# Chunks of the split inputs begin 1088 bytes apart instead of 1024

## The reference, cut to what matters

```python
proj = h @ w_in[l]                                    # and so for each projection
a = jnp.einsum('cd,ced->ce', hc, u[ic])               # PEER, first half
return jnp.einsum('ce,ced->cd', a, v[ic])             # PEER, second half
u, gate_in = jnp.split(hn @ w_in, 2, axis=-1)         # feed-forward
return (jax.nn.gelu(c, approximate=False) * u) @ w_out
```

## Time and profile before

| | |
|---|---|
| runs | 2029.96, 2028.71, 2020.91 us; median 2028.71 |
| span of the profiled execution | 2021.6 us (its time outside the span isn't given; the median is 7.1 us above the span) |
| PE, PEld | busy 1877.1 us (93%), 1800.7 us (89%), 16,518 instructions each |
| DVE, ACT | busy 1456.5 us (72%), 1242.6 us (61%) |
| DMA | 296 MB, mean 146 GB/s |
| mean granted TensorE clock | 0.975 of full speed |

### The profile page before, as it was taken

One profiled execution on the slowest core, in us unless ns is written; L12 is line 12 of the kernel. 1 busy time (PEld: TensorE's weight loads), 2 busy tenths in 40 slices (PEclk: granted clock), 3 DMA queues, 4 the chain that ended last, 5 costly groups with the idle time before them and its releaser, 6 DMA issues. The chain is left out here.

```text
span 2021.6 us, 45016 instructions
## 1 busy us (share of the span) xinstructions
PE 1877.1 (93%) x16518; PEld 1800.7 (89%) x16518; DVE 1456.5 (72%) x3046; ACT 1242.6 (61%) x2420; POOL 0.2 (0%) x4
## 2 busy tenths in 40 slices
PE   8998988999999999999999989687999977999997
PEld 8887888999999976899999989587999976899996
DVE  7667667688985479766666667776888678578857
ACT  5454655777776789655555556733665555666555
POOL 0000000000000000000000000000000000000000
PEclk9999999999999999999999999798999989999998
DMA  6533344466655620266666646101665644166562
GB/s 208 158 97 105 118 143 136 132 194 193 179 186 175 186 84 0 84 194 190 196 191 193 193 139 199 52 3 56 184 196 173 192 126 136 34 190 189 176 198 76
DMA packets 102084, 296.06 MB, mean 146 GB/s; under 512 B 9539, under 2 KB 32454, under 8 KB 101830
## 3 DMA queue, kind: packets, MB, share of 16 engines
q1 hardware_dynamic: 101958, 294.35, 47.0%
HBM read 293.26 MB, written 1.05 MB: 146 GB/s over the span
## 5 line engine op out<-in xcount | busy, mean ns | idle before, releaser
L459 DVE TENSOR_TENSOR w_low<-ring,w_high 128x512 fp32r<-128x512 f32 x1102 | 743.2, 685 | 357.1 <-ACT w_high L453 349.2
L503 PE MATMUL bank<-a_high,w_high 128*128 128x256 f32 x3228 | 921.2, 285 | 74.3 <-DVE w_low L459 39.1
L504 PE MATMUL bank<-a_low,w_high 128*128 128x256 f32 x3228 | 907.5, 281 | 0.0
L505 PE MATMUL bank<-a_high,w_low 128*128 128x256 f32 x3228 | 907.4, 281 | 0.0
L453 ACT ACTIVATE w_high<-ring 128x512 fp32r<-128x512 f32 x1102 | 671.4, 624 | 375.3 <-PE bank L505 372.8
L503 PEld LDWEIGHTS bank<-a_high,w_high 128*128 128x128 f32 x3228 | 620.0, 192 | 90.0 <-DVE w_low L459 39.7
L504 PEld LDWEIGHTS bank<-a_low,w_high 128*128 128x128 f32 x3228 | 616.3, 191 | 0.4
L505 PEld LDWEIGHTS bank<-a_high,w_low 128*128 128x128 f32 x3228 | 616.7, 191 | 0.0
L503 PE MATMUL bank<-s_high,w_high 128*128 128x256 f32 x1024 | 283.5, 277 | 2.0 <-DVE s_low L2446 2.0
L504 PE MATMUL bank<-s_low,w_high 128*128 128x256 f32 x1024 | 283.3, 277 | 0.0
L505 PE MATMUL bank<-s_high,w_low 128*128 128x256 f32 x1024 | 283.3, 277 | 0.0
(11 more groups left out here) (368 smaller groups left out, 1867.8 us busy)
## 6 DMA issues: line engine op xcount, KB each, us to landing
ring<-in_stream SPq DMA_DIRECT2D x273, 512.0 KB, 3.7
ring<-in_peer_u SPq DMA_DIRECT2D x128, 512.0 KB, 3.6
ring<-in_peer_v SPq DMA_DIRECT2D x128, 512.0 KB, 3.5
ring<-in_stream SPq DMA_DIRECT2D x32, 256.0 KB, 3.3
ring<-in_stream SPq DMA_DIRECT2D x12, 192.0 KB, 2.7
x<-in_x SPq DMA_DIRECT2D x4, 256.0 KB, 6.3
arena<-in_mem SPq DMA_DIRECT2D x1, 1024.0 KB, 11.0
out<-x SPq DMA_DIRECT2D x4, 256.0 KB, 2.6
```

Of the source, the lines that this page charges most:

```text
L459: self.nc.vector.tensor_tensor(self.cut(h, self.w_low), self.raw(h), self.cut(h, self.w_high.bitcast(F32)), ALU.subtract)\
L503: self.nc.tensor.matmul(to, lh, rh, start=start, stop=False, **more)
L504: self.nc.tensor.matmul(to, lh, rl, start=False, stop=False, **more)
L505: return self.nc.tensor.matmul(to, ll, rh, start=False, stop=stop, **more)
```

## The change

The row of the tensors for split inputs gets 16 more floats, so that a chunk begins 1088 bytes behind the one before; the views that the kernel uses keep the shape of 256 tokens. 1088 is 2 times 512 and 64 more, so chunks 0 to 7 begin at eight different places modulo 512, 64 bytes apart. The weights' slots are as before. To make place for the longer rows (22 rows of 64 bytes), the arena of the hybrid room gets 256 floats fewer; its scratch moves down by these 1024 bytes.

```diff
+STRIDE = T + 16
-HYBRID_ROOM = 31488
+HYBRID_ROOM = 31232
@@ def pairs(self, chunks):
-        shape = [P, chunks, T]
-        with self.nc.sbuf_tensor(f"a_high{self.rooms}", shape, F32R) as self.a_high, \
-                self.nc.sbuf_tensor(f"a_low{self.rooms}", shape, F32R) as self.a_low:
+        shape = [P, chunks, STRIDE]
+        with self.nc.sbuf_tensor(f"a_high{self.rooms}", shape, F32R) as high, \
+                self.nc.sbuf_tensor(f"a_low{self.rooms}", shape, F32R) as low:
+            self.a_high, self.a_low = high[:, :, 0:T], low[:, :, 0:T]
             yield
@@ def peer(self):
-            with self.nc.sbuf_tensor("s_high", [P, SIDES, T], F32R) as s_high, \
-                    self.nc.sbuf_tensor("s_low", [P, SIDES, T], F32R) as s_low:
-                self.expert_sum(s_high, s_low)
+            with self.nc.sbuf_tensor("s_high", [P, SIDES, STRIDE], F32R) as s_high, \
+                    self.nc.sbuf_tensor("s_low", [P, SIDES, STRIDE], F32R) as s_low:
+                self.expert_sum(s_high[:, :, 0:T], s_low[:, :, 0:T])
```

## The result

| | before | after |
|---|---|---|
| median of four runs | 2028.82 us (2020.91 to 2029.96) | 2065.01 us (2064.09 to 2065.93) |
| ratio | | 1.0173, 95% interval 1.0136 to 1.021 |
| span of the profiled execution | 2021.6 us | 2062.3 us |
| mean granted clock | 0.975 | 0.975 |

A forecast was written before the change was run, and what follows sets the result against it. PE's own pace in the long products was taken to bound the kernel. Instructions, the ACT and DVE writers and PE's streams each counted 0 us, so the time stayed where the runs are: 2027 us, range 2006 to 2056.

The forecast's parts named there:

- the two gears: Lasting paces of PE's matmuls in the long products: fast at 113.3 ns, slow at 117.8 ns, changing where PE has stopped.
- two of its signs: Trace signs named beforehand: PEER's second half slower than 113.3 ns without a stall; a pace going with the chunk's number.
- The second rival: Long fast stretches on PE lose the 113.3 ns pace; whole 30 to 40 us more, 2059 to 2069 us; chance 0.22.
- the choice between the ends: For PE's streams, 0 us was taken between 16.8 us less and at most 40 us more.
- the term of the streams on PE: Effect of the new chunk starts on matmuls streaming while the next weights load; taken as 0 us.
- the last quarter of the loss: Top part of the at most 40 us loss on PE, left out of the range, which stopped at 2056 us.
- The first rival: Slow stretches on PE run at 113.3 ns because shifting relations end a lasting collision; 17 us less, 2012 us; chance 0.26.
- If no stretch at 117.8 is left: Sign in PE's stretches that was to show the slow gear going, 17 us less, as right.
- The second rival's mechanism: On PE, a constant relation keeps streams collision-free; seven of eight new relations put their meeting mid-stream; 30 to 40 us.
- The third rival: Spread starts on PE bring paces below the fast gear, by another 4.45 ns; 74 us less, 1955 us; chance 0.04.
- a draw of gears: A new allocation may bring other gears at some 110 restarts of PE's stream, scattering the time by 6 to 8 us.

The follow-up runs named there:

- low_128: Against the kernel before: a_high and s_high stay at relation -64, a_low and s_low start 128 bytes later, at +64; 2054.26 us, ratio 1.0129.

## Why the prediction was wrong

**Right:** what bounds the kernel, the two gears of the kernel before and their distance of 4.45 ns, that no operation of ACT, DVE or a queue changes, and that a change of pace in the long products would reach the path whole. The sums and the rows hold, and so do two of its signs: PEER's second half left 113.3 ns without a stall, and a pace went with the number of the chunk. The second rival, "the fast gear goes", is what happened, with 2059 to 2069 us for 2065.01 measured. That its 40 us meet the 40.7 of the spans so closely is partly luck: it took 4.45 ns where 5.0 came, gave nothing to the slow stretches, which lost 2.4 us, and counted matmuls outside the long stretches that are fast in no row.

**The step that failed** is the choice between the ends, by which the term of the streams on PE was put at 0: "Whatever tells the gears apart is therefore something in the timing of the start, and the one thing that the change alters is the same in both." The rows were read right: one set of addresses shows both gears. What followed from it was less than I took. It shows that the address does not choose between the two gears; it says nothing on which gears an address allows. The runs showed the term at 35 us in the long stretches alone, of 40.7 us of span: 32.6 us in the fast ones, 5.0 ns for each of some 6,610 matmuls, and 2.4 us in the slow ones. The relation of the kernel before is the only one of the six multiples of 32 tried, modulo 256, where 113.3 is common; of the four that the change visits the other three hardly allow it, and where a place of `s` comes back to the good one for 24 matmuls, the stream stays at 117.8. The prediction even said it: "No row shows another relation under this load". Where no row shows the new state, a forecast of 0 between a bound of -17 and one of +40 us has no support.

**The range** ended at 2056 since it left out the last quarter of the loss. The loss came whole: the new relations took every long stretch out of the fast gear, not a share of them.

**The first rival** (the slow gear goes) nearly holds in the letter: 117.8 is left in one long stretch only, and the sign given for it, "If no stretch at 117.8 is left", would have misled. But the stream moves to 118.3, not to 113.3. That a stream "can't stay in it" was no argument for where it goes.

**The second rival's mechanism** had the right outcome and the wrong geometry: eight relations with one good are in fact four classes modulo 256, visited twice. The good relation holds the slow gear too, so it isn't free of what costs. That the two streams collide is not shown: the runs fix which relations are slow, not what happens in them. **The third rival** (paces below 113.3) has nothing for it: none of the seventeen other kernels profiled, the changed one among them, has a lasting pace under 113.3 ns, so the 109 ns are not reached by this stream at any of these placements. The Trainium skill (TensorE: Matmul & The Clock Gate, "Back-to-back issue gap") gives them for matmuls without the loading of weights between them.

**The scatter** that I ascribed to a draw of gears shows in the runs: the kernel before lay between 2013.35 and 2047.16 us over all comparisons, the kernel at relation 0, with one pace, between 2075.59 and 2079.29, and the changed kernel between 2064.09 and 2065.93.

## What to carry to other kernels

When matmuls stream an input while the next weights load, look at the distance between starts in long stretches; the placement of the two operands relative to each other is a knob that was worth 3% here (2024.55 to 2094.78 us), and two values of that distance in one loop were the hint. Keep the relation constant and try its values with one kernel each, modulo 256 bytes here; rows padded by 64 bytes walk through four of them, and here they lose the fast pace altogether, while rows padded by 256 cost nothing. And a state that exists at one address says nothing about what other addresses allow: where the trace has no row for the new state, keep both bounds in the range.

## What the runs showed of the hardware

- The pace of fp32r matmuls of 256 columns, each with its own weight load, at a granted clock of 1.00, depends on the start of the streamed operand minus that of the loaded one, with the period 256 bytes in the four pairs tried: 113.3 or 117.8 ns at -64, 118.3 at -32, 120.0 at 0, mostly 117.8 at 64, 118.7 at 128, 117.3 to 120.0 at -96; 4 bytes after the best place 120.0 to 122.2 ns, 4 bytes ahead of it 118.6 to 119.8. The Trainium skill (SBUF — State Buffer, "SBUF: two separate sides") counts the two read ports of PE as independent; here their addresses act on each other, and the measurement decides.
- At some relations the pace has several lasting values, taken when the stream starts after a stall and held over more than 3,000 matmuls. What picks the value is open: no kernel was found that is always at 113.3 ns, and why the period is 256 bytes is open too.
- With one matmul in three at a worse relation (`low_128`) no long stretch was at 113.3 ns; the mean of all three was 117.8 ns.
